# Dense attention heads: q and k projected with the tokens moving, rotated per lane and joined by small transfers, in place of token-major projection and transposes

## The reference, cut to what matters

```
qb = rotary(qb.reshape(bsz, lp, 2 * B_HEADS, B_QK_DIM), cos, sin).reshape(bsz, lp, B_HEADS, 2, B_QK_DIM)
kb = rotary(kb.reshape(bsz, lp, 2 * B_HEADS, B_QK_DIM), cos, sin).reshape(bsz, lp, B_HEADS, 2, B_QK_DIM)
# rotary: x1, x2 = the two halves of 32 of a component
#         concatenate([x1 * cos - x2 * sin, x2 * cos + x1 * sin])
s = jnp.einsum('bqhcd,bkhcd->bhcqk', q_blk, k) * scale          # two components c per head, d = 64
p = jax.nn.softmax(s, axis=-1)
a = p[:, :, 0] - lam * p[:, :, 1]
out = jnp.einsum('bhqk,bkhv->bqhv', a, v)
```

## Time and profile before

| | |
|---|---|
| median of 3 runs | 1951.52 us (1950.04 to 1954.15) |
| the profiled execution | 1951.07 us, span of its instructions 1949.8 us |
| PE busy | 1741.2 us (89%), 14474 matmuls |
| PE weight loads | 1621.5 us (83%), beside the matmuls |
| DVE busy | 1143.0 us (59%) |
| ACT busy | 886.3 us (45%) |
| POOL busy | 405.2 us (21%) |
| mean granted TensorE clock | 0.966 of full speed |

### The profile page before, as it was taken

The page is one execution under the profiler, slowest core; times in us unless marked ns, Lnnn a source line. Parts: engine busy times, 40 slices in busy tenths (PEclk is TensorE's granted clock), DMA queues, the critical chain, the costliest instruction groups (busy, mean ns, idle before and its releaser), DMA issues. The chain is left out here.

```text
span 1949.8 us, 37518 instructions
## 1 busy us (share of the span) xinstructions
PE 1741.2 (89%) x14474; PEld 1621.5 (83%) x14474; DVE 1143.0 (59%) x2793; ACT 886.3 (45%) x2700; POOL 405.2 (21%) x390
## 2 busy tenths in 40 slices
PE   3899999999889998978999989999998898988796
PEld 3798998999788787857988989989998787876696
DVE  6475584345457777874175845833554576767615
ACT  4434544345425665663053444452452354656603
POOL 5430221210121001020454203113103001012044
PEclk9899999999989999999999999999998899999998
DMA  7200100100110000032122001011001000003312
GB/s 248 63 26 12 55 23 27 51 25 10 34 45 6 28 10 28 17 130 94 44 95 70 23 12 55 23 32 46 28 10 52 23 9 28 30 8 106 111 62 87
DMA packets 98192, 91.89 MB, mean 47 GB/s; under 512 B 6176, under 2 KB 88336, under 8 KB 98016
## 3 DMA queue, kind: packets, MB, share of 16 engines
q1 hardware_dynamic: 98016, 89.49, 14.1%
HBM read 68.30 MB, written 21.17 MB: 46 GB/s over the span
## 5 line engine op out<-in xcount | busy, mean ns | idle before, releaser
L798 PE MATMUL psum<-w_hi,hT_hi 128*128 128x256 f32 x2400 | 704.0, 293 | 24.3 <-DVE rb L1687 13.7
L798 PE MATMUL psum<-w_hi,hT_lo 128*128 128x256 f32 x2400 | 681.8, 284 | 0.0
L798 PE MATMUL psum<-w_lo,hT_hi 128*128 128x256 f32 x2400 | 681.3, 284 | 0.0
L798 PEld LDWEIGHTS psum<-w_hi,hT_hi 128*128 128x128 f32 x2400 | 459.8, 192 | 36.0 <-DVE rb L1687 16.7
L798 PEld LDWEIGHTS psum<-w_hi,hT_lo 128*128 128x128 f32 x2400 | 459.7, 192 | 0.0
L798 PEld LDWEIGHTS psum<-w_lo,hT_hi 128*128 128x128 f32 x2400 | 459.1, 191 | 0.0
L760 POOL CAST w_hi<-w_raw 128x512 fp32r<-128x512 f32 (+1 forms) x168 | 110.2, 656 | 1377.7 <-DMA w_raw<-in_w_in 813.2
L764 POOL TENSOR_TENSOR w_lo<-w_raw,w_hi 128x512 fp32r<-128x512 f32 (+1 forms) x168 | 211.7, 1260 | 30.9 <-DVE neg_max L1827 19.4
L1826 DVE TENSOR_REDUCE row_max<-psum 128x1 f32<-128x1024 f32 x136 | 165.4, 1216 | 33.7 <-PE psum L938 33.5
L1087 PE MATMUL psum<-vg_b,aT_b 128*128 128x128 f32 (+1 forms) x1224 | 159.4, 283 | 23.3 <-ACT aT_b L1387 23.3
L1087 PEld LDWEIGHTS psum<-vg_b,aT_b 128*128 128x128 f32 (+1 forms) x1224 | 145.3, 189 | 32.2 <-ACT aT_b L1387 28.6
(11 more groups left out here) (161 smaller groups left out, 2677.8 us busy)
## 6 DMA issues: line engine op xcount, KB each, us to landing
w_raw<-in_w_in SPq DMA_DIRECT2D x104, 256.0 KB, 3.7
h_dram<-hbuf SPq DMA_DIRECT2D x16, 512.0 KB, 2.6
w_raw<-in_w_out SPq DMA_DIRECT2D x16, 512.0 KB, 4.1
hbuf<-h_dram SPq DMA_DIRECT2D x16, 512.0 KB, 5.5
qk_b<-y_dram SPq DMA_DIRECT2D x16, 512.0 KB, 3.3
y_dram<-y_stage SPq DMA_DIRECT2D x96, 64.0 KB, 1.6
w_raw<-in_w_in SPq DMA_DIRECT2D x12, 512.0 KB, 4.5
hbuf<-in_x SPq DMA_DIRECT2D x8, 512.0 KB, 7.3
```

The lines of the kernel that those rows point to most:

```text
L798: last = nc.tensor.matmul(out_ap, lhs[a](k), rhs[b](k), start=k == 0 and a + b == 0, stop=k == KT - 1 and b == 1)
```

## The change

The weight columns of the dense q and k are reordered on the host, so that a head's 256 columns are two blocks of 128: block 0 holds the first halves (32) of the components of q and k, block 1 their second halves. A unit is now (f, j): block f of the weights is stationary, and piece j of the tokens (348, 346 or 346 of the 1040) moves; 6 units a head, 24 matmuls each. The result stands with head dimensions on the lanes. DVE rotates whole lanes: for f = 0 two products out of PSUM into `rot`, for f = 1 two more products, a difference and a sum. SP then moves `rot` to `qk_t` in 8 transfers (32 lanes by 346 columns each), which join the halves of a component. ACT rounds all of `qk_t` to `qk_b`, and DVE subtracts. There are no transposes of q and k. `rot` and `qk_t` exist once: the next piece's f = 0 waits until the transfers have landed, the next transfers wait for the last piece's subtraction. In a pass each step makes two halves of a unit while they last. `load_chunk` makes two transfers instead of four for a q-k chunk. A table `rope_t` (128 lanes by 2 by 1040) is loaded in each layer behind group C1.

```diff
 def units(l, g, name):
+    if name == "qk":
+        return [(f, j) for j in range(len(T_PIECES)) for f in range(2)]
...
 def b_steps(l, nx):
     n = q_tiles(l)
-    made = [[] for _ in range(n)]
-    if nx:
-        doubled = TILES - (n - 2)
-        x = 0
-        for t in range(n - 2):
-            for _ in range(2 if t < doubled else 1):
-                made[t].append(x)
-                x += 1
-    return [(t, made[t], made[t - 1] if t else []) for t in range(n)]
+    halves = [(u, half) for u in (units(l, nx, "qk") if nx else []) for half in range(2)]
+    ends = [min(2 * (t + 1), len(halves) - max(n - 3 - t, 0)) for t in range(n)]
+    parts = [halves[a:b] for a, b in zip([0] + ends, ends)]
+    done = [[u for u, half in p if half] for p in parts]
+    return [(t, parts[t], done[t], [j for f, j in done[t - 1] if f] if t else []) for t in range(n)]
...
+        def place_qk(l, g, j):
+            n, w = QK_PIECE[l, g, "qk", j], T_PIECES[j][1]
+            sp.wait_ge(roped, ROPE[l, g, "qk", j])
+            if n > 1:
+                sp.wait_ge(qk_lo_done, n - 1)
+            for half in range(2):
+                for x in range(2):
+                    for c in range(2):
+                        lane, row = 64 * x + 32 * c, 64 * c + 32 * half
+                        sp.dma_start(qk_t[row:row + 32, x, 0:w], rot[lane:lane + 32, half, 0:w]).then_inc(qk_placed, 16)
...
+            group_end(sp, l, "C1")
+            sp.dma_start(rope_sb[:], rope_t).then_inc(rope_in, 16)
             load_chunk(l, "A", "q")
...
             load_chunk(l, "B1", "qk")
+            for j in range(2):
+                place_qk(l, "B0", j)
             load_chunk(l, "B2", "qk")
...
+            place_qk(l, "B0", 2)
+            ahead = {"B0": ("B3", "qk"), "B1": ("O", 0), "B2": ("O", 1)}
+            for g, nx in b_passes(l):
+                for t, _, made, _ in b_steps(l, nx):
+                    for f, j in made:
+                        if f:
+                            place_qk(l, nx, j)
+                    if b_step(l, g, t, -1):
+                        save_y(l, *b_step(l, g, t, -1))
+                    if nx and t == n - 1:
+                        load_chunk(l, *ahead[g])
...
-                if before:
-                    qk_transposes(l, nx, before[0])
                 pe.wait_ge(b_comb, B_STEP[l, g, t])
                 transposes(t, 0)
                 transposes(t, 1)
-                for x in before[1:]:
-                    qk_transposes(l, nx, x)
-                if made:
-                    project(l, nx, "qk", made[0], 0)
+                for x, half in parts[:1]:
+                    project(l, nx, "qk", x, half)
                 transposes(t, 2)
-                if made:
-                    project(l, nx, "qk", made[0], 1)
-                for x in made[1:]:
-                    project(l, nx, "qk", x)
+                for x, half in parts[1:]:
+                    project(l, nx, "qk", x, half)
                 values(t)
...
-        def qk_hi_of(l, g, t):
-            head_hi(("qkT", l, g, t), l, g, "qk", qk_b[:, slot_of(g), 0:2, cols(t)])
+        def qk_hi_of(l, g, j):
+            a, n = T_PIECES[j]
+            act.wait_ge(qk_placed, 16 * 8 * QK_PIECE[l, g, "qk", j])
+            nc.scalar.copy(qk_b[:, slot_of(g), 0:2, a:a + n], qk_t[:, :, 0:n]).then_inc(qk_hi, 1)
...
-                if before:
-                    qk_hi_of(l, nx, before[0])
                 evac_probs(t, 0)
                 evac_probs(t, 1)
-                for x in before[1:]:
-                    qk_hi_of(l, nx, x)
+                for j in before:
+                    qk_hi_of(l, nx, j)
                 if after:
                     exps(after, 0)
...
+        def qk_rope(l, g, u):
+            f, j = u
+            a, n = T_PIECES[j]
+            key = ("unit", l, g, "qk", u)
+            src = psum[:, bank(key), 0:n]
+            cos, sin = rope_sb[:, 0, a:a + n], rope_sb[:, 1, a:a + n]
+            wait_filled(dve, key)
+            if f == 0:
+                if QK_PIECE[l, g, "qk", j] > 1:
+                    dve.wait_ge(qk_placed, 16 * 8 * (QK_PIECE[l, g, "qk", j] - 1))
+                tt(rot[:, 0, 0:n], src, cos, ALU.mult)
+                tt(rot[:, 1, 0:n], src, sin, ALU.mult).then_inc(released[bank(key)], 1)
+                return
+            tt(rot[:, 2, 0:n], src, sin, ALU.mult)
+            then(tt(src, src, cos, ALU.mult))
+            tt(rot[:, 0, 0:n], rot[:, 0, 0:n], rot[:, 2, 0:n], ALU.subtract)
+            tt(rot[:, 1, 0:n], rot[:, 1, 0:n], src, ALU.add).then_inc(roped, 1)
+            dve.wait_ge(roped, ROPE[l, g, "qk", j])
+            release(key)
+        def qk_lo(l, g, j):
+            sl = slot_of(g)
+            a, n = T_PIECES[j]
+            dve.wait_ge(qk_hi, QK_HI[l, g, "qk", j])
+            tt(qk_b[:, sl, 2:4, a:a + n], qk_t[:, :, 0:n], qk_b[:, sl, 0:2, a:a + n].bitcast(F32),
+               ALU.subtract).then_inc(qk_lo_done, 1)
...
                 if after:
                     maximum(after, 0)
-                for x in before[0:1]:
-                    qk_lo(l, nx, x)
-                if after:
                     maximum(after, 1)
-                for x in before[1:]:
-                    qk_lo(l, nx, x)
-                for x in made[0:1]:
+                for j in before:
+                    qk_lo(l, nx, j)
+                for x in made:
                     qk_rope(l, nx, x)
                 if after:
                     combine(after)
-                for x in made[1:]:
-                    qk_rope(l, nx, x)
                 finish(b_step(l, g, t, -1))
```

More of the change, by code:

```diff
@@ L98, in chunk_list @@
     out += [("A", "kv", [(KA, CW)]), ("B3", "vg", b_vg(3)), ("A", "q", [(QA, CW)]), ("A", "g", [(GA, CW)])]
-    out += [(g, "qk", [(QB + P * h, P), (KB + P * h, P)]) for h, g in enumerate(B_HEADS)]
+    out += [(g, "qk", [(QB + 2 * P * h, 2 * P)]) for h, g in enumerate(B_HEADS)]
     out += [("O", c, [(c * CW, CW)]) for c in range(DM // CW)]
@@ L107 @@
 T_TILES = [2, 5, 8]
+T_MAX = max(n for _, n in T_PIECES)
 BESIDE = {("B2", "qk"): "B0", ("B3", "qk"): "B1", ("O", 0): "B2", ("O", 1): "B3"}
@@ L288, in bank_plan @@
             add(("o", l, "A", t), 0)
-        for x in range(TILES):
-            add(("unit", l, "B0", "qk", x), x % 2)
-            add(("qkT", l, "B0", x), 6)
+        for i, x in enumerate(units(l, "B0", "qk")):
+            add(("unit", l, "B0", "qk", x), i % 2)
         for c in range(2):
@@ L295, in bank_plan @@
         for g, nx in b_passes(l):
-            for t, made, before in b_steps(l, nx):
+            for t, parts, _, _ in b_steps(l, nx):
                 if b_step(l, g, t, 1):
@@ L301, in bank_plan @@
                 add(("aT", l, g, t, 1), 1)
-                for x in before:
-                    add(("qkT", l, nx, x), 6)
-                for x in made:
-                    add(("unit", l, nx, "qk", x), 7)
+                for x, half in parts:
+                    if half == 0:
+                        add(("unit", l, nx, "qk", x), 7)
                 add(("aT", l, g, t, 2), 6)
@@ L330 @@
 HEADS_IN = [(l, g, x, t) for l in range(DEPTH) for g, x in [("A", "kv"), ("A", "q")] + [(h, "qk") for h in B_HEADS]
-            for t in units(l, g, x)]
+            for t in (range(len(T_PIECES)) if x == "qk" else units(l, g, x))]
+QK_PIECE = numbered([x for x in HEADS_IN if x[2] == "qk"])
 ROPE = numbered(HEADS_IN)
@@ L503, in build @@
     qk_b = sb(sB, "qk_b", [P, 2, 4, TOK], F32R)
+    rot = sb(sB, "rot", [P, 3, T_MAX])
+    qk_t = sb(sB, "qk_t", [P, 2, T_MAX])
+    rope_sb = sb(sB, "rope_sb", [P, 2, TOK])
     sB.close()
@@ L539, in build @@
     qk_hi = sem("qk_hi")
+    qk_lo_done = sem("qk_lo_done")
+    qk_placed = sem("qk_placed")
+    rope_in = sem("rope_in")
     a_kv_out = sem("a_kv_out")
@@ L711, in _ @@
             load_chunk(l, "B1", "qk")
+            for j in range(2):
+                place_qk(l, "B0", j)
             load_chunk(l, "B2", "qk")
-            for g, ahead in (("B0", ("B3", "qk")), ("B1", ("O", 0)), ("B2", ("O", 1))):
-                for t in range(n):
-                    save_y(l, g, t)
-                    if t == n - 2:
-                        load_chunk(l, *ahead)
-            load_h(l, range(6))
-            for t in range(n):
-                save_y(l, "B3", t)
-                load_y(l, t)
+            place_qk(l, "B0", 2)
[9 more added lines that the diff above has]
+                        load_chunk(l, *ahead[g])
+                    if not nx and t == 0:
+                        load_h(l, range(6))
+                    if not nx and t:
+                        load_y(l, t - 1)
+            save_y(l, "B3", n - 1)
+            load_y(l, n - 1)
             load_h(l, range(6, n))
@@ L1136, in _ @@
             mix_a(l)
-            for x in [*range(TILES), None]:
-                if x is not None:
-                    project(l, "B0", "qk", x)
-                if x != 0:
-                    qk_transposes(l, "B0", TILES - 1 if x is None else x - 1)
```

(22 more changed lines are left out.)

34 lines of the change are left out of this document (15 added, 19 removed).

## The result

The changed kernel takes 1989.7 us (median of 4 runs, 1988.67 to 1992.68), against 1952.84 us for the kernel before on the same chip: ratio 1.0199, 95% interval 1.0186 to 1.0212. It is slower by 37 us, where 35 us less were forecast, and outside the range. The profiled execution took 1988.67 us, its span 1987.4, its mean granted clock 0.945 of full speed (before 0.966). PE is busy for 1736.0 us, hardly less than before, and the chain that ended last names a newcomer.

A forecast was written before the change was run, and what follows sets the result against it. PE was taken to bound projecting steps, the softmax loop the others. Six passes saving 41.7 us and B0's stretches costing 7 gave -34.7 us, from 1951.1 to 1916 us; range 1902 to 1950.

The forecast's parts named there:

- rounding steps: Pass steps behind f = 1, where ACT rounds a piece: 8.65 us each, PE's longer projection covering nearly all the transfers.
- steps with f = 1: Pass steps projecting a piece's second block: 9.1 us, PE waiting 0.6 us because the rotation stands ahead of `combine` on DVE.
- up to the first `combine`, two layers: B0's stretch, where nothing covers the transfers: 3.5 us longer in each layer, 7 us in all.
- 7 x 0.36 + 1.8 = 4.3 us: Placement, from a piece's last sum to all eight transfers landed: SP issues 0.36 us apart, landing 1.8 us after issue.
- the prediction's own slope: Each us of slower transfers counts 24 times: in 18 rounding steps and three times in each B0 stretch.
- the placement becomes the bound: Rival, chance 0.13: slower transfers use up the gain at 5.75 us; at 7.4 us the kernel takes 1990 us.
- signs of being wrong: ACT's transfer wait over 2 us, steps after f = 1 over 10, issues over 0.5 apart, dearer DVE products, B0 over 38.
- The last step of a pass stays: Last step of each of the six passes with a next head: time unchanged by the change.
- The loop that I wrote out: B0's stretch, per piece: transfers 4.3, f = 0 0.97, subtraction 0.91, f = 1 2.0, together 8.2 us.
- no 13 us steps: Sign of being right, in the passes: double steps of 13.1 us vanish, since no step holds more than one unit.
- DVE becomes the bound: Rival, chance 0.10: a piece's six DVE operations are dearer by half, adding 26 us, 1942 us.
- step n-2: The pass step in which the third piece is rounded: forecast 8.65 us.

The follow-up runs named there:

- experiment 2: Changed kernel with only four of a piece's eight transfers made, half of `qk_t` staying zero: 1922.1 us.
- Experiment 3: Changed kernel plus useless PE products in idle time, 72 ahead of B0's meta scores and 24 in the values of step n-2: 1979.1 us.
- experiment 4: Changed kernel with lanes reordered on the host, so ACT copies four blocks in place and SP moves the other four; complete computation: 1922.4 us, ratio 0.9847.
- Experiment 1: Changed kernel without the eight transfers, ACT and DVE reading `rot` directly, halves not joined: 1912.8 us.
- experiment 10: On experiment 4: pieces 0 and 1 rounded late, their f = 1 sum and difference behind `combine`, two of four copies on DVE: 1922.8 us, ratio 0.9832.

## Why the prediction was wrong

Forecast 1916, measured 1989.7. The changed trace is 72.3 us off the forecast sum. By the prediction's own steps:

| step | forecast | measured | adds |
|---|---|---|---|
| rounding steps, 18 | 8.65 us | 10.23 | 28.5 |
| steps with f = 1, 15 | 9.1 us | 9.47 | 5.6 |
| last steps of the six passes | unchanged | 55.0 in sum, now 77.5 | 22.5 |
| the passes' other steps | | | 0.9 |
| up to the first `combine`, two layers | +3.5 each | +12.4, +7.3 | 12.7 |
| B3's passes, the end | 0 | | 2.1 |

**The step that failed first** is the term "7 x 0.36 + 1.8 = 4.3 us". The landing was right (1.9). The issue interval was not: it was 0.62 us, and the placement took 6.35. I took the earlier trace rows's save, because it was nearest in size. Two things were wrong with that. The save is a single issue with none of its kind before it, where the four weight issues beside it (0.535 each) were the only row of issues that *follow each other*. And a transfer from `rot` to `qk_t` is a dearer kind: the first of a group takes 0.51 us where a lone save takes 0.32 to 0.33, and the following ones 0.59. What makes the kind dearer isn't shown; the bytes don't (0.62 us for 22 and 43 KB alike), and the lanes don't (87 KB in 64 lanes are within 0.01 us). No row of the kernel before had this kind in it, and even the weights' row would have given 5.55 us, 0.8 short. I had both ends in the text and chose by size. By the prediction's own slope the 2.05 us are worth 49 us, enough to turn 1916 into 1965. The Trainium skill, page DMA: Bandwidth & Descriptors, section Anatomy of one DMA, gives 2.0 us plus bytes for a transfer that GpSimd issues; SP's transfers here landed after 1.8, 1.9 and 2.1 us for 22, 43 and 87 KB, within 0.3 us of it. By that section alone the sum would have been some 7 us above mine, since it has no interval for SP's issues.

**The slope held.** "Each us counts in 18 rounding steps and three times in each B0 stretch", 24 in all: from 3.8 us (four transfers) to 6.35 that makes 61 us. The two traces differ by 66.6 us (experiment 2), but 16.0 of these lie in the six last steps, where the clock is at work and not the slope; 50.6 are left for the 61, of them 40.6 of 45.9 in the rounding steps. The rival "the placement becomes the bound" gave break-even at 5.75 us, and 6.35 is beyond it; its mechanism is what happened, ACT's wait for `qk_placed` with the exponentials behind it. Its 1990 us is right only by chance: it took 7.4 us of placement and no effect of the clock. With 6.35 it gives 1965. Of the signs of being wrong that the prediction names, four came: ACT's wait over 2 us (2.49), rounding steps over 10, issues over 0.5 apart, a B0 stretch over 38.

**The second failure** is "The last step of a pass stays". I took the clock of the earlier trace rows, 1.00, for a constant. Where PE waits 3.7 us and then works, the trace shows half clock and meta scores of 8.13 us for 4.42, in all six passes 22.5 us. Experiment 3 shows the wait as a cause: with it filled, the last steps lose 15.6 of these 22.5 us, and in one pass the same work runs wholly at the full clock. It is not the only one, since the clock also fell in passes, those of the kernel before among them, where PE had waited less than 1 us. The Trainium skill, page TensorE: Matmul & The Clock Gate, section HAM oscillation — how this bites in real kernels, describes this: waits of the matmul loop on data let the clock fall, and the next work starts slow. This was there to be weighed against a change that adds waits to an engine busy 89% of the time.

**B0's stretch.** The loop that I wrote out (transfers, f = 0, subtraction, f = 1) is the one in the trace, only longer. DVE's timeline, one row for each piece, shows 9.93 us a piece, where my formula with 6.35 in place of 4.3 gives 10.23:

```profile
555.40 0.52 DVE L1829 TENSOR_TENSOR rot<-psum,rope_sb 128x346 f32<-128x346 f32 x1 [6.46 <-DMA qk_t<-rot]
...
565.33 0.52 DVE L1829 TENSOR_TENSOR rot<-psum,rope_sb 128x346 f32<-128x346 f32 x1 [6.36 <-DMA qk_t<-rot]
...
576.05 0.88 DVE L1843 TENSOR_TENSOR qk_b<-qk_t,qk_b 128x692 fp32r<-128x692 f32 x1 [7.15 <-ACT qk_b L1383]
```

The formula gives 38.6 us for the stretch. The measured 40.8 hold about 2.6 us more because the first unit ran at half clock (0.29 us a matmul instead of 0.16), as the work just ahead of it, which the change doesn't touch, did in part in both kernels; in experiment 4 this unit ran at the full clock. So these 2.6 us can't be put down to the change for certain.

**What was right.** The products over 346 columns (0.52 us, forecast 0.52), the rounding (0.77, forecast 0.78), the subtraction (0.88, forecast 0.91), PE's wait for `combine` in steps with f = 1 (0.81, forecast 0.6), no transposes and no 13 us steps. "DVE becomes the bound" fell: its operations cost what I took for them. Experiment 1 shows the rest of the sum as a whole: its span is 38.4 us under the kernel before's. That this is near my 34.7 is partly luck, since my sum has transfers of 4.3 us in it and this run has none. Rounding steps are shorter than I said (8.1) and those with f = 1 longer (9.8), 17.9 for the pair against my 17.75; step n-2 takes 7.5 us instead of 8.65; ahead of the two first `combine`s 3.4 us are saved where I had +7; and the last steps take 62.3 us in sum instead of 55.0.

## What to carry to other kernels

Many small transfers in a row are priced by the interval between issues on their queue, and that is read from a row of issues of the same kind that follow each other, not from a lone one of the right size. Where no trace has such a row, the interval is the term to measure first. Fewer and wider transfers, a second issuing engine, or a data layout in which half of the blocks needn't move each took most of the cost away here. Ask of every wait that a change adds whether an engine's queue has the critical work behind it, and move the waiting instruction behind that work. And treat the clock as part of the sum: a wait of some microseconds on a busy TensorE can be paid twice, and the second time in a step that nobody touched.

## What was unexpected of the hardware

- SP's issue of the y save takes 0.33 us alone and 0.58 behind the eight. A transfer from `rot` to `qk_t` takes 0.51 us as the first and 0.59 behind another (0.63 from start to start), for 22 and for 43 KB; with 87 KB in 64 lanes it is 0.47 and 0.60.
- Now and then a single one of these issues takes 0.95 to 1.73 us, and the rounding of its piece waits for it.
- Eight transfers under way at once from two queues cost no more to land: 1.9 us from SP, 2.0 from ACT in the median.
- Useless matmuls in idle time made the kernel faster: 1922.4 to 1910.7 us, ratio 0.9786 against 0.9847, intervals that don't overlap.
- A copy of 32 lanes by 346 columns takes ACT 0.48 us, about as long as its copy of 128 lanes by 384 (0.46 to 0.48); DVE takes 0.335 us (experiment 10).
